# Issuing nine small loads of each layer from GpSimd instead of ScalarE

## The reference

```python
sh1, sc1, g1, sh2, sc2, g2 = split(silu(cond) @ w_ada[l] + b_ada[l], 6)     # for each group
h = layer_norm_plain(x) * (1 + sc1) + sh1                                   # modulate
proj = h @ w_in[l]                    # q, k, v of attention A; latents c_q, c_kv, k_r; gates
c_q, c_kv = rms_norm(c_q, q_norm), rms_norm(c_kv, kv_norm)
o_na  = attention A   # sample: scores + rpb (position bias), keys = own + cache_na_k, cache_na_v
o_mla = attention B   # sample: keys from c_kv and from cache_mla_ckv, cache_mla_kr
y = (gate_na * (o_na @ w_o_na) + gate_mla * (o_mla @ w_o_mla)) @ w_out
x = layer_norm(ALPHA * x + g1 * y)
h = layer_norm_plain(x) * (1 + sc2) + sh2
logits = h @ router_w + router_b      # top group of 4, top 2 of its 8 experts
x = layer_norm(ALPHA * x + g2 * sum_e combine[e] * (silu(h @ w_gate[e]) * (h @ w_up[e])) @ w_down[e])
```

## Time and profile before

| | us |
|---|---|
| median of three executions | 1130.01 |
| the profiled execution, whole | 1125.36 |
| its span (first to last instruction) | 1123.2 |
| TensorE matmul busy | 960.2 |
| VectorE busy | 318.5 |
| ScalarE busy | 188.4 |
| GpSimd busy | 0.2 |

### The profile page before, as it was taken

One profiled execution on the slowest core, in us unless ns is written; L12 is line 12 of the kernel. 1 busy time (PEld: TensorE's weight loads), 2 busy tenths in 40 slices (PEclk: granted clock), 3 DMA queues, 4 the chain that ended last, 5 costly groups with the idle time before them and its releaser, 6 DMA issues.

```text
span 1123.2 us, 15360 instructions
## 1 busy us (share of the span) xinstructions
PE 960.2 (85%) x6804; PEld 589.4 (52%) x6804; DVE 318.5 (28%) x630; ACT 188.4 (17%) x387; POOL 0.2 (0%) x4
## 2 busy tenths in 40 slices
PE   3399999989839999999829999998983899999983
PEld 1278757777634434343207786677873543434321
DVE  1203322222372212221171142231237322212215
ACT  0002312300012211111110122150001121211111
POOL 0000000000000000000000000000000000000000
PEclk8699999999959999999969999999995899999997
DMA  9666635477895999999764664546596399999990
GB/s 370 227 227 246 230 139 188 155 294 267 352 422 221 426 421 428 429 429 428 336 230 169 244 249 160 180 156 225 195 401 271 151 427 418 429 428 429 428 395 39
DMA packets 43228, 332.99 MB, mean 296 GB/s; under 512 B 5528, under 2 KB 7928, under 8 KB 13968
## 3 DMA queue, kind: packets, MB, share of 16 engines
q1 hardware_dynamic: 33552, 308.82, 68.0%
q10 hardware_dynamic: 9600, 23.07, 6.0%
HBM read 329.38 MB, written 2.49 MB: 295 GB/s over the span
## 4 chain that ended last, share of the span: by engine, by line
PE 75%; DMA 12%; DVE 8%; issue 2%; ACT 1%; ACTq 0%; SPq 0%; DVEq 0%
PE ps L695 15%; PE ps L510 10%; PE ps L708 9%; DMA expert_down<-in_w_dn 5%; PE ps L534 5%; PE ps L625 5%; PE ps L635 4%; PE ps L446 4%; DMA expert_gate_up<-in_w_gu 3%; PE ps L559 3%; PE ps L672 3%; PE ps L460 3%; PE ps L546 3%; PE ps L718 2%; PE ps L591 2%
## 5 line engine op out<-in xcount | busy, mean ns | idle before, releaser
L695 PE MATMUL ps<-expert_gate_up,gatheredT 128*32 128x512 f32 x2048 | 227.3, 596 | 9.8 <-DMA expert_gate_up<-in_w_gu 9.0
L695 PEld LDWEIGHTS ps<-expert_gate_up,gatheredT 128*32 128x32 f32 x2048 | 69.2, 110 | 156.9 <-issue 156.8
L708 PE MATMUL ps<-expert_down,hiddenT 128*32 128x512 f32 x1024 | 115.2, 595 | 9.7 <-issue 5.0
L510 PE MATMUL ps<-hT,dense 128*128 128x256 f32 x512 | 114.2, 381 | 0.0
L510 PEld LDWEIGHTS ps<-hT,dense 128*128 128x128 f32 x512 | 96.1, 190 | 16.0 <-issue 3.6
L1332 DVE TENSOR_TENSOR hidden<-hidden,ps 128x256 f32<-128x256 f32 x32 | 13.5, 421 | 224.7 <-ACT hidden L953 224.7
L1342 DVE SCALAR_TENSOR_TENSOR y_lo<-ps,slot_weight,y_hi 128x512 fp32r<-128x512 f32 x64 | 48.1, 751 | 93.5 <-ACT y_hi L965 93.5
L708 PEld LDWEIGHTS ps<-expert_down,hiddenT 128*32 128x32 f32 x1024 | 32.2, 109 | 80.5 <-issue 50.9
L460 PE MATMUL ps<-const,h_tokens 128*128 128x128 f32 x64 | 14.7, 422 | 68.1 <-DVE h_tokens L1048 68.1
L446 PE MATMUL ps<-dense,cond 128*32 128x256 f32 x768 | 54.9, 408 | 17.0 <-ACT cond L831 9.4
L534 PE MATMUL ps<-hT,dense 128*128 128x256 f32 x256 | 57.3, 382 | 2.5 <-DVE hT L999 2.5
(11 more groups left out here) (190 smaller groups left out, 958.0 us busy)
## 6 DMA issues: line engine op xcount, KB each, us to landing
expert_gate_up<-in_w_gu SPq DMA_DIRECT2D x64, 2048.0 KB, 19.1
expert_down<-in_w_dn SPq DMA_DIRECT2D x64, 1024.0 KB, 15.7
dense<-in_w_ada SPq DMA_DIRECT2D x48, 1024.0 KB, 4.9
dense<-in_w_in SPq DMA_DIRECT2D x28, 1024.0 KB, 6.3
dense<-in_w_o SPq DMA_DIRECT2D x8, 1024.0 KB, 6.2
dense<-in_w_out SPq DMA_DIRECT2D x8, 1024.0 KB, 6.9
shift<-ada_rows ACTq DMA_DIRECT2D x4, 1024.0 KB, 12.4
scale<-ada_rows ACTq DMA_DIRECT2D x4, 1024.0 KB, 8.0
```

Source lines behind the costliest of these rows:

```text
L510: last = mm(b[:, m * 256:(m + 1) * 256], w[:, k, m * P:(m + 1) * P], hT[:, k, :], start=(k == 0), stop=(k == KD - 1))
L695: last = mm(ps[r:r + 32, q, :], xgT[:, k, s, at_:at_ + CAP], w_gu[(i * EPI + 2 * q + j) % SLOTS][:, k, :], start=(k == 0), stop=(k == KD - 1),
L708: last = mm(ps[32 * e:32 * e + 32, 2 + c, :], hidT[:, e // 2, f, at_:at_ + CAP], w_dn[(i * EPI + e) % SLOTS][:, f, c * 512:(c + 1) * 512], ...
```

## The change

The nine loads of a layer get a GpSimd program of their own, with the same order, the same sources and destinations and the same semaphores. GpSimd waits for `layer_done` only in layer 1, so in layer 0 it can issue the seven loads of `small_in` at once, where ScalarE came to them after `ada_load` of the scale. The two loads of `kvc_in` still wait for `h_ready`. ScalarE keeps its own waits for `layer_done` and `h_ready`.

```diff
+        @block.gpsimd
+        def _(pool):
+            for l in range(DEPTH):
+                if l:
+                    pool.wait_ge(layer_done, l)
+                pool.dma_start(bias[:, :, :], io["rpb"][l]).then_inc(small_in, 16)
+                pool.dma_start(ckvcT[:, :, :], io["ckvT"][l]).then_inc(small_in, 16)
+                pool.dma_start(krc[:, :], io["kr"][l]).then_inc(small_in, 16)
+                pool.dma_start(qn[:, :], dram(io["q_norm"], l * QL, [[0, P], [1, QL]])).then_inc(small_in, 16)
+                pool.dma_start(kvn[:, :], dram(io["kv_norm"], l * KVL, [[0, P], [1, KVL]])).then_inc(small_in, 16)
+                pool.dma_start(rw[:, :, :], io["router_w"][l]).then_inc(small_in, 16)
+                pool.dma_start(rb[:, :], dram(io["router_b"], l * (NG + NE), [[0, P], [1, NG + NE]])).then_inc(small_in, 16)
+                pool.wait_ge(h_ready, 4 * l + 2)
+                pool.dma_start(kcT[:, :, :], io["kcT"][l]).then_inc(kvc_in, 16)
+                pool.dma_start(vc[:, :], io["vc"][l]).then_inc(kvc_in, 16)
...
         @block.scalar
...
                 if l:
                     act.wait_ge(layer_done, l)
-                act.dma_start(bias[:, :, :], io["rpb"][l]).then_inc(small_in, 16)
-                act.dma_start(ckvcT[:, :, :], io["ckvT"][l]).then_inc(small_in, 16)
-                act.dma_start(krc[:, :], io["kr"][l]).then_inc(small_in, 16)
-                act.dma_start(qn[:, :], dram(io["q_norm"], l * QL, [[0, P], [1, QL]])).then_inc(small_in, 16)
-                act.dma_start(kvn[:, :], dram(io["kv_norm"], l * KVL, [[0, P], [1, KVL]])).then_inc(small_in, 16)
-                act.dma_start(rw[:, :, :], io["router_w"][l]).then_inc(small_in, 16)
-                act.dma_start(rb[:, :], dram(io["router_b"], l * (NG + NE), [[0, P], [1, NG + NE]])).then_inc(small_in, 16)
                 sqrt(l, 0, 2)
                 act.wait_ge(h_ready, 4 * l + 2)
-                act.dma_start(kcT[:, :, :], io["kcT"][l]).then_inc(kvc_in, 16)
-                act.dma_start(vc[:, :], io["vc"][l]).then_inc(kvc_in, 16)
```

## The result

The changed kernel takes 1135.64 us, the median of 20 executions (1130.4 to 1139.13), beside 1130.41 us for the kernel before (20 executions, 1123.94 to 1139.04). The ratio is 1.0038, 95% interval 1.0023 to 1.0053: +4.3 us, between 2.6 and 6.0. (It is taken over all executions; the two medians differ by 5.2 us.) That is inside the 0.5% that the prediction called no change and inside its range (1127.0 to 1136.0), and above the +1.05 us of its sum. The change is a small loss.

What follows compares the result with a forecast made beforehand. TensorE carries 75% of the chain; layer 0's first 47 us are transfers, with DMA engines full until 36 us. Terms 0 - 0.53 + 1.58 + 0 + 0 = +1.05 us gave 1131.1 us, range 1127.0 to 1136.0.

Steps and rivals of the forecast that it cites:

- upper bound: Layer 0: if the engines lose no time, the scale can't be later than by about 3.0 us.
- part 2: Both layers: ScalarE's copy of transposes starts sooner without two issues ahead, ending TensorE's 0.26 and 0.27 us idle; -0.53 us.
- GpSimd holds VectorE: Rival, layer 1: GpSimd's issuing holds up VectorE, +5.4 to +8.0 us in all, 1135.4 to 1138.0 us; chance 0.13.
- part 5: Layer 1, 582.15 to 589.11 us: GpSimd issuing beside VectorE costs 0, or at most 6.96 us; taken as 0.
- Part 1: Both layers: ScalarE's issues ahead of the square root are hidden behind VectorE's work or wait; worth 0.
- Part 3: Layer 0: seven loads move to the front, delaying the w_ada stream but freeing the scale; net +1.58 us.
- The cost term: Layer 0 front: the seven loads need 3.65 us of full DMA engines, delaying w_ada, shift and store; +3.65 us.
- The give-back: Layer 0: the scale, without small loads behind it, lands in 5.0 us instead of 7.07; -2.07 us.
- Part 4: Layer 1: bytes move at the same time, and slower GpSimd issues up to 3.0 us each stay covered; cost 0.
- The rival that the front is free: Layer 0: the seven loads slip between others in the first 9 us; -2.6 us, 1127.4 us; chance 0.17.
- The rival that GpSimd is late: Layer 0: slowly prepared loads spread to 36 us, still ahead of the scale; +1 us; within the forecast's 0.65.
- the change is worth part 2 and no more: By the skill's rule that all issuers share sixteen DMA engines, spreading loads saves only issuing time; -0.5 us.

Runs made afterwards that it cites:

- e6: Kernel before, with ScalarE issuing all nine loads of a layer after its two copies of transposed tokens, no GpSimd; ratio 0.9995 to the kernel before.
- e1: Kernel before, with layer 0's seven small loads issued at the front by ScalarE, right behind x_res; ratio 1.0041 to the kernel before.
- e7: As e1, but ScalarE issues layer 0's seven loads after silu(cond), so its issues don't delay cond; ratio 1.0012 to the kernel before.
- e11: Changed kernel, with layer 0's seven loads issued twice by GpSimd, first on a semaphore nobody waits for; ratio 1.0058 to the kernel before.
- e12: Changed kernel, but in layer 0 GpSimd waits until const and cond_in have landed before the seven loads; ratio 1.0033 to the kernel before.
- e2: Changed kernel, but in layer 0 GpSimd waits for the second row's store, the loads' old time; ratio 1.0003 to the kernel before.
- e3: Changed kernel, but in layer 0 GpSimd waits until the scale and shift have landed; ratio 1.0004 to the kernel before.
- e5: Kernel before, with only the keys and values moved to GpSimd, the seven small loads staying on ScalarE; ratio 1.0001 to the kernel before.
- e8: e6 plus SyncE holding back w_in pieces and everything behind them until layer 0's shift and scale have landed; ratio 0.9965 to the kernel before.

## Why the prediction was right or wrong

**The range: met by luck; the sum: too small.** It said +1.05 us and it is +4.3 (2.6 to 6.0). The forecast's own mechanism had an upper bound: with the scale 3.0 us late and the 0.53 us of part 2 off, about 1132.5 us (1130.01 + 3.0 - 0.53). The measured 1135.64 lies above it, where the range reached only because it took in the near end of the rival that GpSimd holds VectorE (1135.4). The time alone would speak for that rival, and the traces rule it out (part 5).

**Part 1, ScalarE's issues ahead of the root: right.** Worth 0 in both layers. e6 keeps them on ScalarE elsewhere and loses nothing that can be told; in layer 1 VectorE's stretch is the same.

**Part 2, the copy: right in sum.** From the start of the second h_tokens product to the projection, before took 6.06, 6.24, 6.24 us in layer 0 and 6.47, 6.56, 6.56 in layer 1; the changed kernel's two profiles show 6.10, 6.11 and 6.10, 6.29. On the means -0.41 us, against -0.53: 0.08 of it in layer 0 and 0.33 in layer 1, so the whole came out and the even split did not. Layer 0's difference is smaller than the scatter of before.

**Part 3, the front: the mechanism right, both terms mis-sized.** e1, e7, e11 and e12 put bytes in front by either issuer and are slower or, like e7, lean that way; e2, e3 and e6 put them elsewhere and are not. The scale was issued at 41.85 us, not at the 39.5 that the prediction named, and landed in 5.4 us as it said.

The cost term was 3.65 us; the second row moved from 30.6 to 35.9 us on the means, 5.3 us. The row it was sized from the earlier trace rows had only the scale and the end of the shift beside the small loads. In front they mix with pieces of `w_ada`, and the whole stream moves less: from 3 to 36 us the kernel before moved (12 x 413 + 12 x 399 + 9 x 411) / 1000 = 13.44 MB, the kernel after (12 x 398 + 12 x 378 + 9 x 374) / 1000 = 12.68 MB, at the same full share. The 0.76 MB that went missing are 1.9 us at 410 GB/s, beside 2.8 us for the 1.165 MB themselves: 4.7 of the 5.3 us.

The slower stream is measured; how much of it the loads cause is not settled. By the same sum the other profile of the changed kernel moved 12.61 MB, e7 and e12 12.83 each, but e2, e5 and e3, which had nothing in front, 12.86, 13.03 and 13.10, beside 13.26 to 13.55 in e6 and the three profiles of before. That small packets slow it is argued only.

The give-back was 2.07 us; store and scale together, from the second row to h_tokens, went from 13.2 to 11.6 us on the means, 1.6 us. The bound of 3.0 us did not hold: the scale landed 3.8 us later on the means. It took for granted that the engines lose no time.

**Part 4, loads that come late: right.** GpSimd needs 0.54 us an issue, and in both profiles of the changed kernel the mask addition waits for no load in either layer. In e6, where it waited until 57.00 us, nothing that can be told was lost.

**Part 5 and the rival that GpSimd holds VectorE: right to take 0.** VectorE's instructions in layer 1 have their old lengths while GpSimd issues, and the stretch from `layer_done` to the transposes is 6.95 us in all five profiles of the two kernels. The Trainium skill (*SBUF — State Buffer*, the box on the trap that VectorE blocks a DMA) states that a 2-port instruction of VectorE keeps GpSimd from writing descriptors; nothing of the kind shows here, with the products at their 2.47 us and GpSimd's issues at 0.54 us beside them. In which mode they ran no run tells.

**What the steps did not have.** The first projection took 9.49 and 9.05 us in the changed kernel and 7.15, 7.14, 8.72 before, 1.6 us more on the means. The chain of waits shows it:

```profile
56.09 9.49 PE ps L551 x32
```

The long form is the clock. The matmuls are the same; in the third profile of the kernel before the granted clock is still at 0.50 (1.2 GHz) from 54 to 57 us, with 8 of them in these 3 us, where the first profile has 1.00 (2.4 GHz) and 16:

```profile
54.00:57.00 3.00, 3.00 (x8) 2.34 (x9) 0.58 (x1) 0.00 (x0) 0.00 (x0) 0.50 0.00 0
```

```profile
54.00:57.00 3.00, 3.00 (x16) 2.64 (x15) 0.00 (x0) 0.00 (x0) 0.00 (x0) 1.00 0.00 0
```

The changed kernel's first profile has the same 8 in 3 us, from 57 to 60 us, though its record of the clock reads 1.00 there (last section).

With the terms above, 5.3 - 1.6 - 0.4 + 1.6 = +4.9 us, inside the measured 2.6 to 6.0. Whether this last term belongs to the change is open: with loads in front 5 of 6 profiles have the long form (e12 not), without 3 of 8 (the third of before, e2, e8). In layer 1, where the loads kept their time, the same projection took 7.14, 8.81 and 9.15 us in the three profiles of before and 7.15 and 9.39 in the changed kernel's two, so it scatters by as much without the change.

**The rival that the front is free: fell.** It had 0.17; the engines had no gap, as their share said.

**The rival that GpSimd is late: fell.** Its seven issues in front ended at 5.1 us. That the change is worth part 2 and no more, -0.5 us, fell as well: the bytes moved to the front cost more than that.

## What to carry to other kernels

Before moving a load "out of the way" of an issuing engine, look at whether the DMA engines are full where it will land: an issue of 0.5 us is cheap, the megabyte in front of the chain is not. An early start for data that is needed late can be a loss, and holding back a prefetch until a small dependent store and load have gone through gained more (0.35%) than any choice of issuer. And take two or three profiles of a kernel before sizing a term of 1 us from one.

## What the runs showed of the hardware

A DMA issued by GpSimd took 0.54 us of its time, whatever its size (16 to 512 KB), the first one of the execution 0.67 us. In e11 GpSimd issued seven back to back and the eighth only 16.7 us later. On q10 the nine loads of a layer made 144 packets each on the mean ((9600 - 7008) / 18), on q0 64 each (1152 / 18), for the same bytes. GpSimd began the first issue after `h_ready` 0.5 us after ScalarE acted on the same semaphore value (602.14 beside 601.64 us). The 4 KB store of the second row landed after 4.0 to 7.2 us with other loads under way, and after 1.58 us when the engines were idle (e8).

In the kernel after, the granted clock reads 1.00 from 57 to 60 us, while TensorE got through 8 matmuls of the projection in these 3 us, 0.37 us each, against 16 in 3 us (54 to 57) before: there the clock's record does not follow what the matmuls show.
